# Six borders of a three-block transformer kernel: an earlier seal on the buffers, the last three weight units by tile of tokens, and the norms of the third and fourth tile in turn

## The reference, cut to what matters

```python
# block 1
x = layer_norm(ALPHA * x + 0.5 * swiglu(x, ...), ln1_g, ln1_b)     # border "ffn1"
mix = hybrid_mixer(x, w_in, ...)                                   # attention + SSD, @ w_out
x = layer_norm(ALPHA * x + mix, ln2_g, ln2_b)                      # border "out1"
x = layer_norm(ALPHA * x + 0.5 * swiglu(x, ...), ln3_g, ln3_b)
# block 2
y = hybrid_mixer_2(rmsnorm(h, mix_pre_g), ...)                     # border "norm2" lies before it
h = h + rmsnorm(y, mix_post_g)
y = conv_gated_ffn(rmsnorm(h, ffn_pre_g), ...)                     # border "out2" lies before it
h = h + rmsnorm(y, ffn_post_g)
# block 3
h = rmsnorm_3(x, norm1_g) * (1 + sc1) + sh1                        # border "down2"
x = x + gt1 * hybrid_mixer_3(h, ...)
h = rmsnorm_3(x, norm2_g) * (1 + sc2) + sh2                        # border "out3"
x = x + gt2 * (square(relu(h @ mlp_w1)) @ mlp_w2)
return rmsnorm_3(x, final_g)
```

## Time and profile before

| | |
|---|---|
| time, median of 3 runs | 3874.12 us (3867.44 to 3878.79) |
| time of the profiled execution | 3863.07 us |
| its span, first to last instruction | 3861.8 us |
| instructions | 44288 |
| TensorE matmul busy | 3595.6 us |
| VectorE busy | 2050.9 us |
| ScalarE busy | 1398.2 us |
| GpSimd busy | 388.0 us |
| mean granted TensorE clock | 0.971 |

### The profile page before, as it was taken

How to read it: one execution, slowest core, us unless ns; L and a number is a source line. 1 busy time by engine, 2 the same in 40 slices (tenths; PEclk the granted TensorE clock), 3 DMA queues, 4 the chain that set the end, 5 groups by cost and what they waited for, 6 DMA issues and landing times. The chain is left out here.

```text
span 3861.8 us, 44288 instructions
## 1 busy us (share of the span) xinstructions
PE 3595.6 (93%) x17148; PEld 2923.2 (76%) x17148; DVE 2050.9 (53%) x3283; ACT 1398.2 (36%) x2423; POOL 388.0 (10%) x362
## 2 busy tenths in 40 slices
PE   8999899988999999989999989998999998988999
PEld 7877777876777787766887778877776677877877
DVE  4446465769436323741343466657365475562256
ACT  2224243321523223526223353345344232342244
POOL 1000000026000100003000100000000113121101
PEclk9999999989999999989999999999999999999999
DMA  6545311210223323520222232344301220132255
GB/s 234 182 170 180 97 50 55 88 46 23 82 94 120 115 93 120 178 78 1 99 79 81 77 103 95 96 159 135 107 28 37 76 82 12 34 120 77 93 177 167
DMA packets 106126, 380.16 MB, mean 98 GB/s; under 512 B 11760, under 2 KB 14592, under 8 KB 105792
## 3 DMA queue, kind: packets, MB, share of 16 engines
q1 hardware_dynamic: 100944, 364.86, 28.5%
q0 software_dynamic: 2896, 10.38, 0.8%
q10 hardware_dynamic: 2080, 2.10, 0.2%
HBM read 375.19 MB, written 2.10 MB: 98 GB/s over the span
## 5 line engine op out<-in xcount | busy, mean ns | idle before, releaser
L396 DVE TENSOR_TENSOR w_low<-ring,w_high 128x1024 fp32r<-128x1024 f32 (+1 forms) x637 | 814.7, 1281 | 1002.9 <-ACT w_high L384 979.2
L420 PE MATMUL bank<-x_low,w_high 128*128 128x512 f32 (+1 forms) x2560 | 1006.4, 397 | 89.1 <-DVE w_low L396 49.8
L420 PE MATMUL bank<-x_high,w_low 128*128 128x512 f32 (+1 forms) x2560 | 993.5, 392 | 0.0
L384 ACT ACTIVATE w_high<-ring 128x1024 fp32r<-128x1024 f32 (+1 forms) x637 | 670.3, 1053 | 875.7 <-PE bank L420 381.7
L420 PEld LDWEIGHTS bank<-x_low,w_high 128*128 128x128 f32 x2560 | 499.2, 195 | 195.3 <-issue 56.2
L420 PE MATMUL bank<-x_high,w_high 128*128 128x512 f32 (+1 forms) x2560 | 636.1, 387 | 0.0
L420 PEld LDWEIGHTS bank<-x_high,w_low 128*128 128x128 f32 x2560 | 499.8, 195 | 98.4 <-issue 1.4
L420 PEld LDWEIGHTS bank<-x_high,w_high 128*128 128x128 f32 x2560 | 467.0, 192 | 99.3 <-issue 1.9
L480 PE MATMUL bank<-w_low,x_high 128*128 128x512 f32 (+3 forms) x416 | 156.8, 377 | 1.3 <-ACT z_z L1647 1.3
L482 PE MATMUL bank<-w_high,x_high 128*128 128x512 f32 (+3 forms) x416 | 155.5, 374 | 0.0
L481 PE MATMUL bank<-w_high,x_low 128*128 128x512 f32 (+3 forms) x416 | 155.4, 374 | 0.0
(11 more groups left out here) (624 smaller groups left out, 5726.7 us busy)
## 6 DMA issues: line engine op xcount, KB each, us to landing
ring<-in_W SPq DMA_DIRECT2D x688, 512.0 KB, 3.5
f_hid<-in_xT ACTq DMA_DIRECT2D x2, 1024.0 KB, 11.8
X<-in_x POOLq DMA_DIRECT2D x1, 2048.0 KB, 10.0
out<-X SPq DMA_DIRECT2D x4, 512.0 KB, 4.1
const<-in_consts POOLq DMA_DIRECT2D x1, 1389.0 KB, 6.2
f_norm<-in_ln_g POOLq DMA_DIRECT2D x2, 512.0 KB, 8.0
f_norm<-in_ln_b POOLq DMA_DIRECT2D x2, 512.0 KB, 10.0
ring<-in_W SPq DMA_DIRECT2D x2, 432.0 KB, 3.0
```

What stands on the lines that cost most here:

```text
L384: ac.activation(b.UH[i % NU][:, 0:src.shape[1]], src, ACT.Copy).then_inc(*b.split.act.up("high", i))
L396: dv.tensor_tensor(b.UL[i % NU][:, 0:n], src, b.UH[i % NU][:, 0:n].bitcast(F32), SUB).then_inc(*b.split.dve.up("low", i))
L420: i = pe.matmul(out, w[:, k, c], v, start=n == 0 and q == 0, stop=last and q == 3 * K - 1)
```

## The change

It has three parts at each of the six borders, and one of them reaches the last down stage too.

1. **Seal.** TensorE's seal of the six stages moves ahead of half 1: what is sealed is the turn of tile 3.
2. **Last three units by tile.** In pass p = 1, `tensor_down` does all units but the last three (`NU`) as before. For those it goes first over tile 2 with all three units, then over tile 3 with all three. The units are released by tile 3's matmuls, one by one. The turn of a tile that was placed after one of these units (out1, out2, out3) now comes after tile 3's matmuls of it.
3. **Stagger.** Tile 2's norm is done to its end, then tile 3's, instead of step by step for both. On TensorE the turn of tile 2 moves ahead of the third unit of half 0 (`between`). `scalar_ahead` and `vector_ahead` of the border move behind a part of tile 2's norm.

```diff
-def tensor_first(b, g, keys, banks, half, ready):
+def tensor_first(b, g, keys, banks, half, ready, between=None):
...
     for key, bank in zip(keys, banks):
+        if between and key == keys[-1]:
+            between()
...
 def tensor_down(b, g, d, p, emptied):
...
-    for k in range(d.nk):
+    last = d.nk - NU if p else d.nk
+    for k in range(last):
...
+            tensor_down_tile(b, g, d, banks, i, t)
         yield k
+    for t in (2 * p, 2 * p + 1) if p else ():
+        for k in range(last, d.nk):
+            i = p * d.nk + k
+            if t == 2 * p:
+                pe.wait_ge(*g.dve.at("in_low", d.tag, i))
+                tensor_await(b, (d.tag, i))
+            tensor_down_tile(b, g, d, banks, i, t)
+            if t != 2 * p:
+                yield k
...
 def scalar_ln_end(b, g, key):
+    scalar_norm_root(b, g, 2)
     scalar_ahead(b, key)
-    for t in (2, 3):
-        scalar_norm_root(b, g, t)
+    scalar_norm_root(b, g, 3)
...
 def vector_ln_end(b, g, sums, G, rows, key):
     for t in (2, 3):
         sums(t)
         vector_norm_stats(b, g, t, [g.dve.at("sum", t, 1)])
+        vector_norm_apply(b, g, t, G, rows)
         if t == 2:
             vector_ahead(b, key)
-    for t in (2, 3):
-        vector_norm_apply(b, g, t, G, rows)
...
+    scalar_post_kept(b, g, d.tag, 2, Y)
+    scalar_post_square(b, g, 2, Y, sq)
+    scalar_post_root(b, g, 2)
+    scalar_post_kept(b, g, d.tag, 3, Y)
+    scalar_ahead(b, key)
+    scalar_rms_square(b, turn, 2, [g.dve.at("x", 2)])
+    scalar_rms_root(b, turn, 2)
+    scalar_post_square(b, g, 3, Y, sq)
+    scalar_post_root(b, g, 3)
+    scalar_xn_turn(b, turn, 2)
+    scalar_rms_square(b, turn, 3, [g.dve.at("x", 3)])
+    scalar_rms_root(b, turn, 3)
+    scalar_xn_turn(b, turn, 3)
...
+    vector_post_mean(b, g, 2)
+    vector_post(b, g, 2, Y, G, gsem)
+    vector_ahead(b, key)
+    vector_rms_mean(b, turn, 2)
+    vector_rms_scale(b, turn, 2)
+    vector_post_mean(b, g, 3)
+    vector_post(b, g, 3, Y, G, gsem)
+    vector_rms_mean(b, turn, 3)
+    vector_rms_scale(b, turn, 3)
     for t in (2, 3):
         vector_xn_turn(b, turn, t)
...
     for t in (2, 3):
         scalar_rms_square(b, turn, t, [g.pool.at("sum", t, 1)])
         scalar_rms_root(b, turn, t)
+        if t == 2:
+            scalar_ahead(b, key)
...
-    vector_gated_sum(b, g, d.tag, 2, GT, tmp)
-    vector_ahead(b, key)
-    vector_gated_sum(b, g, d.tag, 3, GT, tmp)
     for t in (2, 3):
+        vector_gated_sum(b, g, d.tag, t, GT, tmp)
         vector_rms_mean(b, turn, t)
         vector_rms_scale(b, turn, t)
+        if t == 2:
+            vector_ahead(b, key)
     for t in (2, 3):
         vector_xn_turn(b, turn, t)
...
-    tensor_qkv1_first(b, m1, 0, x_turned(p.f1.turn))
-    for t in (2, 3):
-        tensor_x_turn(b, p.f1.turn, t)
+    tensor_qkv1_first(b, m1, 0, x_turned(p.f1.turn), lambda: tensor_x_turn(b, p.f1.turn, 2))
+    tensor_x_turn(b, p.f1.turn, 3)
+    b.seal("ffn1", "pe")
     tensor_qkv1_first(b, m1, 1, x_turned(p.f1.turn))
-    b.seal("ffn1", "pe")
```

More of the change, by code:

```diff
@@ L547, in vector_down, with tensor_down_tile @@
         yield k
+def tensor_down_tile(b, g, d, banks, i, t):
+    pe, k, u = b.nc.tensor, i % d.nk, d.H[i % d.n]
+    wh, wl = b.halves((d.tag, i))
+    s = slice(128 * (t % 2), 128 * (t % 2) + 128)
+    for h in range(2):
+        c, out = slice(512 * h, 512 * h + 512), banks[t, h].ap
+        if k == 0:
+            for e in banks[t, h].emptied:
+                pe.wait_ge(*e)
+        pe.matmul(out, u[:, 0, s], wl[:, 0, c], start=k == 0, stop=False)
+        pe.matmul(out, u[:, 1, s], wh[:, 0, c], start=False, stop=False)
+        x = pe.matmul(out, u[:, 0, s], wh[:, 0, c], start=False, stop=k == d.nk - 1)
+        if k == d.nk - 1:
+            x.then_inc(*g.pe.up(d.tag, "row", t, h))
+    if k < d.nk - 1 and t % 2:
+        x.then_inc(*g.pe.up(d.tag, "part", i))
 def tensor_down(b, g, d, p, emptied):
@@ L791, in ffn_emptied, with tensor_ffn_first @@
     return s.g.act.at("silu", j) if what == 0 else s.g.dve.at("hid", j)
-def tensor_ffn_first(b, s, half, ready):
+def tensor_ffn_first(b, s, half, ready, between=None):
     if half == 0:
         s.banks = [b.bank((s.tag, m), ffn_emptied(s, m)) for m in range(3)]
-    tensor_first(b, s.g, [(s.tag, m) for m in range(3)], s.banks, half, ready)
+    tensor_first(b, s.g, [(s.tag, m) for m in range(3)], s.banks, half, ready, between)
 def tensor_ffn(b, s):
@@ L1153, in mix1_units, with tensor_qkv1_first @@
     down_units(b, s.gw, s.down, "w_out")
-def tensor_qkv1_first(b, s, half, ready):
+def tensor_qkv1_first(b, s, half, ready, between=None):
     if half == 0:
         s.banks = [b.bank(("q1", m), s.gq.act.at("q", m)) for m in range(3)]
-    tensor_first(b, s.gq, [("q1", m) for m in range(3)], s.banks, half, ready)
+    tensor_first(b, s.gq, [("q1", m) for m in range(3)], s.banks, half, ready, between)
 def tensor_qkv1(b, s):
@@ L1812, in scalar_post_square @@
         ac.activation(Y[:, t, h * 512:(h + 1) * 512], b.bk[tag, t, h], ACT.Copy).then_inc(*g.act.up("kept", t, h))
+def scalar_post_square(b, g, t, Y, sq):
+    ac = b.nc.scalar
     ac.wait_ge(*g.act.at("kept", t, 1))
@@ L1941, in q2_emptied, with tensor_qkv2_first @@
     return s.gq.act.at("q", m) if m < 4 else s.gq.dve.at("k", m)
-def tensor_qkv2_first(b, s, half, ready):
+def tensor_qkv2_first(b, s, half, ready, between=None):
     if half == 0:
         s.banks = [b.bank(("q2", m), q2_emptied(s, m)) for m in range(3)]
-    tensor_first(b, s.gq, [("q2", m) for m in range(3)], s.banks, half, ready)
+    tensor_first(b, s.gq, [("q2", m) for m in range(3)], s.banks, half, ready, between)
 def tensor_qkv2(b, s):
@@ L2554, in ffn2_units, with tensor_ffn2_first @@
     down_units(b, s.gd, s.down, "ffn_w_down_2")
-def tensor_ffn2_first(b, s, half, ready):
+def tensor_ffn2_first(b, s, half, ready, between=None):
     if half == 0:
         s.banks = [b.bank(("c2u", m), s.g.act.at("copied", m)) for m in range(3)]
-    tensor_first(b, s.g, [("c2u", m) for m in range(3)], s.banks, half, ready)
+    tensor_first(b, s.g, [("c2u", m) for m in range(3)], s.banks, half, ready, between)
 def tensor_ffn2(b, s):
@@ L2764, in q3_emptied, with tensor_qkv3_first @@
     return s.gq.act.at("q", m) if 2 <= m < 6 else s.gq.dve.at("k", m)
-def tensor_qkv3_first(b, s, half, ready):
+def tensor_qkv3_first(b, s, half, ready, between=None):
     if half == 0:
         s.banks = [b.bank(("q3", m), q3_emptied(s, m)) for m in range(3)]
-    tensor_first(b, s.gq, [("q3", m) for m in range(3)], s.banks, half, ready)
+    tensor_first(b, s.gq, [("q3", m) for m in range(3)], s.banks, half, ready, between)
 def hidden_steps(b, s):
@@ L3755, in gated_parts, with tensor_mlp_first @@
     return lambda t, h: g.dve.at("part", t, h)
-def tensor_mlp_first(b, s, half, ready):
+def tensor_mlp_first(b, s, half, ready, between=None):
     if half == 0:
         s.banks = [b.bank(("f3u", m), s.gm.act.at("relu", m)) for m in range(3)]
-    tensor_first(b, s.gm, [("f3u", m) for m in range(3)], s.banks, half, ready)
+    tensor_first(b, s.gm, [("f3u", m) for m in range(3)], s.banks, half, ready, between)
 def tensor_mlp(b, s):
```

78 lines of the change are left out of this document (18 added, 60 removed).

## The result

The changed kernel takes 3833.53 us (median of 4, 3831.84 to 3840.37) against 3876.11 on the same chip: ratio 0.9897, interval 0.9877 to 0.9918. Run again later it took 3836.72 against 3866.30: 0.9918, 0.9905 to 0.9931. So it is 0.8 to 1.0% faster, 32 to 40 us, where I had forecast 0.65%.

A forecast was written before the change was run, and what follows sets the result against it. TensorE, busy 93% of the span, was taken as the bound, with only its idle time and slow clock to win. -33.6 - 12.4 + 3.0 + 19.2 - 1.3 = -25.1 us, giving 3838.0 (3849 against the median), range 3836 to 3865.

The forecast's parts named there:

- The gaps: Behind half 1 at the borders: waits of 34.6 us shrink to 0.95 at down2, a gain of 33.6 us.
- The echo: The six 6 us windows behind those waits: the slow clock of 0.54 to 0.74 goes, a gain of 12.4 us.
- Part 2's stalls: Down stages of out1 and out2: waits of some 4 and 3 us, each with slow clock after, 3.0 us in all.
- Half 1 later: Six borders, down stage's end to half 1: half 1 starts later, 19.2 us in all.
- The six chains: Hand-added waits from norm to half 1: later by 2.0, 3.1, 5.7, 2.7, 0.6, 5.1 us (ffn1, out1, norm2, out2, down2, out3).
- The port: ffn1, out1, norm2: low part waits beside GpSimd's shift, 3.4 us; rival: VectorE keeps its port, 1.2 us, 3844, chance 0.12.
- The stagger of the post and gated borders: At out3, tile 2 takes 7.3 us from gated sum to scaled tile; half 1 comes 5.1 us later.
- The tail: Kernel's end: GpSimd's four sums start 2.8 us earlier and the last ends 1.3 us sooner.
- the gaps did not stay: Rival: next stage's work still held until half 1 ends, seal gives nothing, 20.9 us slower, 3895; chance 0.06.
- no border paid 5.7 us: Rival: third unit is the victim at every border, each pays norm2's 5.7 us, 3864 in all; chance 0.15.
- The stagger costs nothing: Rival: tile 2 gets ahead of the weights in the queues, so 47 us less, 3827; chance 0.08.

The follow-up runs named there:

- e1: The kernel before with only TensorE's six seals moved ahead of half 1: 3824.42 us, ratio 0.9875 to the kernel before.
- e4: The kernel before with the moved seals and the last three units by tile, without the stagger: 3839.96 us, ratio 0.9919 to the kernel before.
- e5: e3 with TensorE turning tile 2 behind the whole of half 0 at all six borders: 3822.56 us, ratio 0.9886 to the kernel before.
- e8: The changed kernel run once more, unaltered: 3836.72 us, ratio 0.9918 to the kernel before.
- e3: The changed kernel with the old order of units in the down stages, so seal and stagger only: 3818.05 us, ratio 0.9862 to the kernel before.
- e7: e3 with VectorE summing tile 3 ahead of the next low part of weights at ffn1, out1 and norm2: 3821.57 us, ratio 0.9881.
- e11: The changed kernel with VectorE summing tile 2 ahead of the second unit's low part at ffn1, out1 and norm2: 3832.33 us, ratio 0.9904.
- e2: The changed kernel with TensorE's six seals back behind half 1: 3874.41 us, ratio 1.0011 to the kernel before.
- e6: The changed kernel with the order by tile in the last down stage alone: 3816.95 us, ratio 0.9871 to the kernel before.
- e9: e6 with tile 2 turned behind the whole of half 0 at norm2 alone: 3817.61 us, ratio 0.9862 to the kernel before.
- e10: e3 with the order by tile in the down stages of 22 and 32 units only: 3819.92 us, ratio 0.9871 to the kernel before.
- e12: e3 run once more, unaltered: 3817.41 us, ratio 0.9864 to the kernel before.

## Why the prediction was right, and where it was off

The direction and its cause were right: the seal's wait goes, with its echo, and a part of that is given back. The time fell 7 to 15 us more than forecast: half 1's later start was priced far too high, with the wrong sign for the stagger, the stalls in the down stages were priced too low, and half 1's own length was not in the sum. By the prediction's terms (profiled executions, before and after):

- *The gaps, −33.6.* Measured 34.6 to 0.8, −33.8. Right, with the places: I had 0.95 left at down2, and 0.55 is left there and 0.23 at out2. GpSimd's loads do start with half 1 at ffn1.
- *The echo, −12.4.* The six windows have clock 1.00, so the full 12.4. Gaps and echo together, −46.2, are part 1 alone, which measured −46 to −48.
- *Not in the sum: half 1 itself.* 66.1 to 60.2, −5.9 us. With the turn of tile 2 ahead of the third unit, that unit stands between the long wait and the last one, and half 1 begins at a higher clock. The kernels without the early turn (e1, e4, e5) have 64.3 to 65.2 us, those with it at all six borders 57.5 to 62.7. I had priced the clock of the third unit (2.2 and its like) as a loss and not seen that it is taken off half 1.
- *Part 2's stalls, +3.0.* The waits are there, 4.17 us at out1 and 3.04 at out2 (I had "some 4" and 3), each followed by slow matmuls. But my sum took in only the slow clock behind them and not the waits. Beside those of the kernel before, 4.8 us of waiting are new at these two, 1.3 more at out3, and the slow matmuls cost 4.0. The three stages grew by 10.4 us, 9.4 in e8.
- *Half 1 later, +19.2.* This is the step that failed: S grew by 1.4 us and not by 19.2. By border it is 0.0, −1.3, +2.9, −1.0, −0.3 and +1.1 (ffn1, out1, norm2, out2, down2, out3), where I had 2.0, 3.1, 5.7, 2.7, 0.6 and 5.1. The six chains hold two things. One is the later start of the norms by part 2: 1.4 three times, 2.5 twice and 2.9, 12.1 us. It measured 5.6 (e4 less e1) or 7.4 (e8 less e3); at out1 and out2 hardly any of it is in S (0 and 0 by the first pair, 0.8 and 0.2 by the second), it lies in the longer stage ahead. The other is the stagger, the remaining 7.1 us. It has the wrong sign: e3 less e1 is −6.5, and e5 shows that −5.0 of it is the order of the norms. Between before and e3 norm2 alone got longer, by 2.0 where I had 4.3; the other five got 0.9 to 2.1 us shorter each. At ffn1 the wrong wait can be named. I had tile 2's turn wait for the bank (3, 1) until 11.2 us behind the down stage's end. It began 9.9 us behind it, when GpSimd's shift was done, and tile 3's sum had emptied the bank 1.1 us before that:

```profile
418.41 0.34 PE L605 MATMUL bank<-const,X 128*128 128x128 f32 x1 [2.03 <-POOL X L747]
```

  Two of the chains are also added up wrongly, by 0.2 us at norm2 (1660.2 and not 1660.4) and 0.5 at out3 (3488.2 and not 3488.7). Which waits were wrong at the other borders I have not worked out.
- *The port*, inside that term. I took 3.4 us for a low part beside GpSimd's shift, because of the earlier trace rows, and gave the other order a chance of 0.12. It took 1.22 at all three borders, and GpSimd's shift 3.2. Priced as in that rival, this is 4.6 us of the miss. The Trainium skill, "SBUF — State Buffer", section "Who interferes with whom", gives the pair to whoever issues first; the traces agree in both orders (e7). Norm2's old row, on which I leaned, shows a limit of reading this from starts: there VectorE's normalising starts at 1651.15 and GpSimd's shift at 1651.20, and VectorE waited all the same (2.96, against 0.81 for tile 2's). Starts 0.05 us apart don't tell who is first (the last item has two more such pairs); 0.26 apart, as in the changed kernel, they did.
- *The stagger of the post and gated borders.* At out3 tile 2 went from its gated sum to the scaled tile in 5.9 us (3446.89 to 3452.78) and tile 3 was scaled 7.0 later, where I had 7.3 and 7.9: GpSimd's two sums took 2.52 together, where I had 1.6 each. The four groups of turned columns end it, as I had it, 8.1 us.
- *The tail, −1.3.* From the last matmul's end to the kernel's end it was 9.5 us before and 8.4 in the changed kernel's profile, which looks like a hit. It is luck. Of the eight profiled executions with part 2 in the last stage two have 8.4, this one and e11; in e2, e4, e6, e8, e9 and e10 it is 9.5 again. The port decides, at the end of e8:

```profile
3828.56 1.29 DVE L3849 SCALAR_TENSOR_TENSOR X<-X,small,f_norm 128x1024 f32<-128x1024 f32 x1
3828.65 2.32 POOL L3773 TENSOR_TENSOR X<-X,f_tmp 128x512 f32<-128x512 f32 x1
```

VectorE's gain of tile 2, which nobody waits for, holds up GpSimd's last sum (1.27 us undisturbed), which everything waits for. In the first profile of the changed kernel GpSimd's last sum, the second of the two in the first line, kept its 1.26 us (from 3832.05) and VectorE waited, although VectorE's gain started 0.06 us ahead of it here and 0.09 us ahead in e8:

```profile
3830.82 2.49 POOL L3773 TENSOR_TENSOR X<-X,f_tmp 128x512 f32<-128x512 f32 x2 [1.72 <-DVE f_tmp L3766]
3831.99 2.40 DVE L3849 SCALAR_TENSOR_TENSOR X<-X,small,f_norm 128x1024 f32<-128x1024 f32 x1
```

The sum by the measured terms of the profiled execution: −33.8 − 12.4 − 5.9 + 10.4 + 1.4 − 1.1 = −41.4; the ratios give −32 to −40. The profiled execution's −22.7 has 10.7 us of slow pace in it (c2d 125.6 to 129.8 us, f3d 179.3 to 185.9), which leaves −33.4. Most of the other 8 us lie in one stretch, from the unit behind down2's half 1 to out3's down stage, before and after:

```profile
2697.59:3416.46 718.87, 651.74 (x3521) 528.70 (x3521) 411.93 (x944) 251.12 (x583) 92.65 (x115) 0.96 0.17 55
2666.34:3389.72 723.38, 656.30 (x3521) 533.55 (x3521) 412.31 (x944) 252.12 (x585) 92.50 (x115) 0.96 0.17 55
```

It is 4.5 us longer, where the echo alone should have made it 1.9 shorter. The matmuls are the same 3521, and TensorE is busy with them for 4.6 us longer. The other thirteen profiled executions all have 721.0 to 725.7 us there, e1 and e2 too; with only one profiled execution of the kernel before, whether its 718.9 was luck stays open.

For the rivals: the port kept by VectorE came true, the gaps did not stay, and no border paid 5.7 us. "The stagger costs nothing" is true of part 3 (e3), which even gains, and not of part 2. That leaves the price of each part: part 1 −48, part 3 −5 (e3 against e1), part 2 +13 to +21 (the changed kernel's two ratios against e3 and e12), of which only some 2.5 by the times, and 5 by S, come from the long stages. Parts 2 and 3 together cost 4 us without the seal (e2) and 9 to 17 with it (the changed kernel's two ratios against e1). The traces show no such difference in what the parts themselves do: S, 8-unit stages and half 1 together are 5.7 us longer in e2 than before, and 5.5 longer in e8 than in e1. What e8 has besides is the slow pace of its last stage, 185.8 us against e1's 178.0; the last section comes back to it.

## What to carry to other kernels

A release that guards more than it must is found in the view of waits, and its gap has an echo in the clock that can be priced beside it: together they were the whole gain here. Finishing rows earlier by reordering a reduction holds the buffers of its last units longer; with 22 or 32 units per pass that cost some 2.5 us in all (5 in S), with 8 it cost 10 to 18, so it is to be asked what else waits for those buffers. And before a chain is priced at its slowest row, look at which of the two engines in that row was issued first.

## What the runs showed of the hardware

**Two paces at full clock.** Windows of 20 us inside c2d's down stage, of e3 and of e12, which are the same kernel; the number behind PE's busy time counts matmuls, and the clock is 1.00 in both:

```profile
2520.00:2540.00 20.00, 20.00 (x88) 16.23 (x88) 11.52 (x15) 9.64 (x15) 0.00 (x0) 1.00 0.57 193
```

```profile
2520.00:2540.00 20.00, 20.00 (x86) 15.89 (x84) 10.77 (x15) 9.40 (x15) 0.00 (x0) 1.00 0.55 177
```

One runs at 0.231 us a matmul and the other at 0.240, for tens of us at a stretch and with hardly anything between the two. It came in c2d in four of the fourteen profiled executions (the changed kernel's, e5, e10, e12), in the last stage in four (the changed kernel's, e8, e9, e11) and once in ffn1's (e5). It costs 3 to 11 us of an execution. The four of the last stage are among the eight with the order by tile there, and none is among the six without it; but e2, e4, e6 and e10 have that order and the faster pace. So the order doesn't bring it by itself, whether it makes it likelier is open, and so is what sets it.

**The clock of half 1 goes with the work between the waits before it.** At norm2 the same 72 matmuls took 8.9 us at 1.00 in e12 and 10.9 at 0.79 in e9. A wait of 3 us stands right before them in both; before that come 7.1 us of work behind a wait of 7.88 in e12, and 3.7 us of work behind one of 4.29 in e9.
